# Four weight chunks of a Trainium2 decoder block laid 4160 instead of 4096 bytes apart

## What is computed

```
proj = rmsnorm(x) @ w_in                     # 2048 x 13848
mkv  = rmsnorm(mem) @ w_mem_kv               # 2048 x 2048
merged = bgate0*(y_a @ w_br_nsa) + bgate1*(y_b @ w_br_ret) + bgate2*(y_c @ w_br_mem)
x = x + rmsnorm(merged @ w_o)
u = causal_dwconv(rmsnorm(x) @ w_up, conv_w, conv_b)     # 2048 x 11264
x = x + rmsnorm((gelu(u_gate) * u_val) @ w_down)         # 5632 x 2048
```

## Time and profile before

| what | value |
|---|---|
| median of 3 runs | 1696.08 us |
| lowest and highest | 1695.91 and 1696.55 us |
| profiled execution, its own time | 1696.61 us |
| span of the profiled execution | 1694.8 us |
| mean granted TensorE clock | 0.999 of full |
| TensorE busy | 1685.0 us, 99% |
| VectorE busy | 1128.4 us, 67% |
| ScalarE busy | 830.7 us, 49% |
| DMA | 327.95 MB, 194 GB/s, 62% of the DMA engines' span |

### The profile page before, as it was taken

The page is one execution under the profiler, slowest core; times in us unless marked ns, Lnnn a source line. Parts: engine busy times, 40 slices in busy tenths (PEclk is TensorE's granted clock), DMA queues, the critical chain, the costliest instruction groups (busy, mean ns, idle before and its releaser), DMA issues.

```text
span 1694.8 us, 24997 instructions
## 1 busy us (share of the span) xinstructions
PE 1685.0 (99%) x8842; PEld 1453.6 (86%) x8842; DVE 1128.4 (67%) x1534; ACT 830.7 (49%) x1139; POOL 49.6 (3%) x55
## 2 busy tenths in 40 slices
PE   9999999999999999999999999999999999999998
PEld 8888899998888888888888888888888888888886
DVE  7755576767575544554565787677776786776777
ACT  7544455544434444444444665555455455554453
POOL 1000000000140000000000000000000000000000
PEclk9999999999999999999999999999999999999999
DMA  9576478445656667666557556565565665665564
GB/s 293 183 246 203 133 237 262 117 147 174 211 162 185 195 192 210 201 195 190 185 188 245 180 188 198 181 199 195 187 202 171 190 210 186 190 195 176 189 199 148
DMA packets 241917, 327.95 MB, mean 194 GB/s; under 512 B 12907, under 2 KB 159116, under 8 KB 241292
## 3 DMA queue, kind: packets, MB, share of 16 engines
q1 hardware_dynamic: 241804, 326.47, 62.0%
HBM read 321.71 MB, written 3.67 MB: 192 GB/s over the span
## 4 chain that ended last, share of the span: by engine, by line
PE 94%; DMA 2%; DVE 2%; ACT 1%; issue 1%; POOL 0%; POOLq 0%; DVEq 0%; ACTq 0%
PE bank L1532 22%; PE bank L1523 16%; PE bank L1521 16%; PE bank L1522 16%; PE bank L1541 12%; PE bank L1552 2%; DMA wraw<-in_cmp_w_v 1%; PE bank L1557 1%; PE bank L1496 1%; PE bank L1495 1%; PE bank L1497 1%; DVE wlo L930 1%; DMA wraw<-in_cmp_w_k 1%; ACT whi L614 1%; PE bank L1721 0%
## 5 line engine op out<-in xcount | busy, mean ns | idle before, releaser
L930 DVE TENSOR_TENSOR wlo<-wraw,whi 128x1024 fp32r<-128x1024 f32 x584 | 708.0, 1232 | 450.3 <-ACT whi L614 291.2
L614 ACT ACTIVATE whi<-wraw 128x1024 fp32r<-128x1024 f32 x584 | 614.1, 1058 | 548.5 <-PE bank L1523 389.7
L1532 PE MATMUL bank<-hx,whi 128*128 128x512 f32 x1504 | 350.7, 390 | 0.0
L1532 PEld LDWEIGHTS bank<-hx,whi 128*128 128x128 f32 x1504 | 280.0, 188 | 57.0 <-DVEq L1053 0.2
L1521 PE MATMUL bank<-whi,hx 128*128 128x512 f32 x512 | 201.6, 394 | 0.0
L1523 PE MATMUL bank<-whi,hx 128*128 128x512 f32 x512 | 199.4, 389 | 0.0
L1522 PE MATMUL bank<-wlo,hx 128*128 128x512 f32 x512 | 199.2, 389 | 0.0
L1541 PEld LDWEIGHTS bank<-hx,wlo 128*128 128x128 f32 x1504 | 186.9, 192 | 3.7
L1541 PE MATMUL bank<-hx,wlo 128*128 128x256 f32 x1504 | 188.7, 283 | 0.0
L1521 PE MATMUL bank<-whi,r_hi 128*128 128x512 f32 x384 | 149.8, 390 | 0.0
L1522 PE MATMUL bank<-wlo,r_hi 128*128 128x512 f32 x384 | 149.5, 389 | 0.0
(11 more groups left out here) (275 smaller groups left out, 1799.8 us busy)
## 6 DMA issues: line engine op xcount, KB each, us to landing
wraw<-in_w_in SPq DMA_DIRECT2D x200, 512.0 KB, 4.0
wraw<-in_w_up SPq DMA_DIRECT2D x176, 512.0 KB, 4.5
wraw<-in_w_down SPq DMA_DIRECT2D x88, 512.0 KB, 4.7
wraw<-in_w_mem_kv SPq DMA_DIRECT2D x32, 512.0 KB, 4.8
wraw<-in_w_o SPq DMA_DIRECT2D x32, 512.0 KB, 4.3
wraw<-in_w_br_mem SPq DMA_DIRECT2D x16, 512.0 KB, 4.3
wraw<-in_w_br_nsa SPq DMA_DIRECT2D x16, 512.0 KB, 4.3
wraw<-in_w_br_ret SPq DMA_DIRECT2D x16, 512.0 KB, 4.4
```

The costliest lines, as they stand in the source:

```text
L614: nc.scalar.activation(whi[:, c], wraw[:, c], ACT.Copy).then_inc(hi_done, 1)
L930: V.tensor_tensor(wlo[:, c], wraw[:, c], whi[:, c].bitcast(F32), ALU.subtract).then_inc(lo_done, 1)
L1532: e = T.matmul(ps[pair[u]][:, :], whi[:, c, k, u * P:(u + 1) * P], x2[:, :, 4 * c + k, :], start=c == 0 and k == 0, stop=False, skip_group ...
```

## The change

The tensor `whi` becomes 4352 words per partition instead of 4096, and its four chunks start 1040 words (4160 bytes) apart instead of 1024 words (4096 bytes). So against `wraw`, `wlo` and the activations, chunks 0 to 3 are shifted by 0, 64, 128 and 192 bytes. `wlo` and everything declared behind `whi` start 1024 bytes later. Each chunk is still 1024 contiguous words, and no instruction is added, removed or moved.

```diff
+HIGH_PITCH = CK * GW + 16
...
         wraw = sb("wraw", [P, 4, CK, GW])
-        whi, wlo = (sb(n, [P, 4, CK, GW], F32R) for n in ("whi", "wlo"))
+        high = sb("whi", [P, 4 * CK * GW + 256], F32R)
+        whi = high[:, 0:4 * HIGH_PITCH].rearrange("p (c n) -> p c n", c=4)[:, :, 0:CK * GW].rearrange("p c (k n) -> p c k n", k=CK)
+        wlo = sb("wlo", [P, 4, CK, GW], F32R)
         arena = sb("arena", [P, 12288])
```

## The result

The changed kernel takes 1719.68 us (median of 4 runs, 1719.32 to 1721.91), the kernel before 1695.99 us (4 runs, 1695.75 to 1696.55). The ratio is 1.0142, 95% interval 1.0124 to 1.0160: 23.7 us slower, far outside the forecast range of 1694.3 to 1697.8. The profiled execution of the changed kernel took 1719.75 us with a span of 1718.0 us.

A forecast was written before the change was run, and what follows sets the result against it. TensorE's back-to-back matmuls were taken to bound the kernel. The profiled 1696.61 us plus 0 from all terms, with bounds -1.6 and +0.9 us, gave 1696.1 us against the median; range 1694.3 to 1697.8 us.

The forecast's parts named there:

- What bounds the kernel: Whole kernel: TensorE is busy 1685.0 of 1694.8 us, so only the distance between matmul starts or new TensorE waits could matter.
- instructions, ScalarE, VectorE, start and end: Terms outside TensorE's matmuls: nothing added or moved, L614 and L930 unchanged and covered by TensorE, 0 us each.
- I take 0 ns per matmul: TensorE reading shifted `whi` in 3108 matmuls: the shift was claimed to cost or give nothing.
- the gate columns: Matmuls at L1736 and L1737, read as running through the change's own shifts at 119.7 ns each, against 120.0 ns aligned.
- the bounds of -0.9 and +0.9 us: On the 3108 shifted matmuls: 0.3 ns each, from the gate columns' mean below and the reading error above.
- Rival B: L1521, L1523, L1532, L1552, chunks 1 to 3: shifted slices cost 6.6 ns a matmul, 20.5 us, giving 1716.6 us; chance 0.03.
- the disturbed stretch of the earlier trace: Where `chunk_w` begins after a second pass: three distances in 0.70 us, 233 ns instead of 226.7, the slower rival's price.
- the 3108: Matmuls with `whi` as operand that meet a shift, counted as three quarters of 4144.
- a fixed cost of 13.3 ns beside the columns: Every matmul of 256 or 512 columns: its columns at 2.4 GHz plus about 13.3 ns.
- Rival A: The regular 13.3 ns is a collision of operand reads that the shift removes: at the limit 41.3 us less, 1654.8 us; chance 0.04.

The follow-up runs named there:

- The sweep: TensorE alone, the reference's computation left out, operands shifted row by row: with 512 columns 226.9 ns unshifted, 233.1 at 64 bytes; with 256 columns 119.8 and 113.5 ns.
- part (b) of the second sweep: TensorE alone, the reference's computation left out; stationary and moving operand shifted in turn by 64 bytes, in step or crossed: 231.7 and 231.5 ns.

## Why the prediction was wrong

**What bounds the kernel** was right. TensorE never stops; a loop step is matmuls of 226.7 and 120.0 ns; nothing but the distance between starts could matter. That instructions, ScalarE, VectorE, start and end add 0 us was right too: L614's and L930's total busy times differ by under 1.5 us (614.2 and 709.2 us after), TensorE's waits are 1.8 us in all, and moving what lies behind by 1024 bytes costs nothing.

**The step that failed** is the sentence "I take 0 ns per matmul", from the gate columns. It failed in three ways.

- *The shape.* The gate columns have 256 moving columns, and their mean of 119.7 ns was carried over to 512. The sweep has both: at 256 columns no shift of the change costs anything (113.5 ns at 64 bytes), at 512 the same shifts cost 6.2, 5.6 and 2.3 ns.
- *The shifts.* The reading took the step of 192k bytes and left out where `wg` itself starts. Between `tables` and `wg` stand `work`, `eye`, `stack`, `gain`, `conv` and `wgr`, with 10240, 512, 224, 192, 1408 and 1536 bytes, so `wg` starts 32 bytes behind a multiple of 256, counted from `hx`. The relative starts there are 32, 224, 160 and 96, and none is a shift of the change.
- *The mean.* It hid what the single starts show. Two stretches of three distances:

```profile
47.17 0.29 PE L1736 MATMUL bank<-hx,wg 128*128 128x256 f32 x1
...
47.54 0.28 PE L1737 MATMUL bank<-hx,wg 128*128 128x256 f32 x1
47.66 0.28 PE L1736 MATMUL bank<-hx,wg 128*128 128x256 f32 x1
...
48.00 0.28 PE L1737 MATMUL bank<-hx,wg 128*128 128x256 f32 x1
```

They take 0.37 and 0.34 us. Without the rounding, the 30 distances run from 113 to 127 ns, while inside a second pass each is 120 after the first few. So the gate columns were an irregular sequence that happened to come out near 120 ns, and the bounds of -0.9 and +0.9 us, drawn from their mean, were no bounds for matmuls of another shape. Rival B even says that no row shows a shifted moving operand; it was priced and then given 0.03.

**The price.** Rival B gave 1716.6 us and was the right mechanism: place L1521, L1523, L1532 and L1552, 6.6 ns a matmul, taken from the disturbed stretch of the earlier trace rows. The measured time is 1719.68 us, but B came so near in part by luck, since two terms were off, one against the other. The lines that read `whi` lost 17.2 us (first passes 6.2 and 0.5, L1521 5.5, L1523 4.5, L1552 0.5) where B had 20.5: 5.4 ns on each shifted matmul instead of 6.6. (There are 3204 of them; the 128 matmuls of L1532 that read `mx` were left out of the 3108.) And L1522 with its unshifted `wlo`, which B had at nothing, lost 7.0 us. Together this is 24.2 us; the matmuls of 256 columns gave a little back (0.7 us at L1541). That stretch of the earlier trace rows was also the hint that was missed: the distance between starts is not a fixed cost of 13.3 ns beside the columns, it can be 233 ns where no operand is shifted, as in the first matmuls behind a second pass.

**Rival A** (the shift removes the 13.3 ns) is out for 512 columns, where nothing under 226.6 ns was seen. For 256 columns it was half right, though the change touches few of those: 6.7 of the 13.3 ns can go. The page "TensorE: Matmul & The Clock Gate" in the Trainium skill, section "Back-to-back issue gap", has about 2.5 ns beside the columns for isolated matmuls; no run here came down to it, the lowest steady means were 226.7 and 113.3 ns.

**Open.** Why the relative start matters is not shown. The runs say that TensorE alone is enough, that the shifts tried beyond 256 bytes repeat those below (320, 384 and 448 bytes have 233.3, 232.5 and 229.2 ns), and that the disturbance spreads to neighbours. Which reads meet was tried in part (b) of the second sweep and is not settled.

## What to carry to other kernels

Where TensorE is the bound, with a weight load ahead of every matmul and 512 moving columns, keep the starts of the stationary and the moving operands equal modulo 256 bytes, for neighbouring matmuls too, and on multiples of 32 bytes, pads and pitches included. Here steps of 64 bytes in one buffer cost 1.4 to 1.9%. Evidence on such an effect holds only for the shape that it was seen in: 256 and 512 moving columns answered in opposite ways. When a row is taken as evidence on placement, count its addresses from the first tensor, and look at its single distances, not at their mean. Before laying out buffers, let TensorE alone run the kernel's own order of operands at every shift: that predicted the second pass's 3.64 us exactly, while a row in another order promised three times the gain that came.

## What the runs showed of the hardware

- A 128x512 fp32r matmul behind its own weight load starts 226.7 ns after the one before if all operands start alike modulo 256 bytes and on multiples of 32, and 233.1, 232.5 and 229.2 ns on average if the stationary one starts 64, 128 or 192 bytes further on. Starts that are alike but an odd multiple of 16 bytes gave 230 to 231 ns.
- The cost belongs to the sequence, not to the single matmul: L1522, with no shifted operand, lost 7.0 us between two shifted neighbours, and matmuls whose own operands start alike had 231.7 ns when every second one lay 64 bytes further on.
- With 256 columns some shifts do the opposite: 120.0 ns aligned, on average 113.5 ns at 64 bytes in one order of operands, and 113.8 ns at 76 bytes in the kernel's (113.3 ns once steady).
- The "SBUF — State Buffer" page of the Trainium skill, section "Who interferes with whom", gives TensorE two independent read ports and has it wait on nobody. No other engine disturbed it here: the aligned distances, 226.7 and 120.0 ns, are the same in the kernel and with TensorE alone. But with every other engine idle the relative place of its own two operands moved its pace by 3% at the change's shifts, and by 5% at the worst (164 bytes, 237.5 ns).
